# Earlier small loads, rearranged routing and no barrier around an untaken branch in a two-layer trunk on eight cores

## The reference, cut to what matters

```python
h = x * (1 + scale) + shift                      # rows of c @ ada_w + ada_b
x = layer_norm(alpha * x + (1 + gate) * mixer_or_moe(h), g, b)
# MoE
g_p, g_idx = top_k(softmax(h @ w_group + b_group), 1)
sel = expert_logits of group g_idx               # 8 per token
top_vals, top_idx = top_k(sel, 2)
w = softmax(top_vals) * g_p
y = sum over the two experts of w * (silu(h @ gate) * (h @ up)) @ down
```

## Time and profile before

| what | us |
|---|---|
| median of 3 runs | 2430.23 (2411.65, 2430.23, 2433.24) |
| profiled execution, its own time | 2433.36 |
| span of its slowest core (core 2) | 2432.3 |
| spans of the 8 cores | 2382.4 to 2432.3 |
| mean granted clock of TensorE, share of full | 0.77 to 0.78 |
| busy, core 2: PE, DVE, ACT, POOL | 1298.3, 1240.6, 640.7, 439.5 |
| DMA moved, core 2 | 413 MB |

### The profile page before, as it was taken

The page is one execution under the profiler, slowest core; times in us unless marked ns, Lnnn a source line. Parts: engine busy times, 40 slices in busy tenths (PEclk is TensorE's granted clock), DMA queues, the critical chain, the costliest instruction groups (busy, mean ns, idle before and its releaser), DMA issues.

```text
span 2432.3 us, 30523 instructions; the slowest of 8 cores (2382.4 to 2432.3 us)
## 1 busy us (share of the span) xinstructions
PE 1298.3 (53%) x9485; PEld 805.2 (33%) x9627; DVE 1240.6 (51%) x2415; ACT 640.7 (26%) x1257; POOL 439.5 (18%) x565
## 2 busy tenths in 40 slices
PE   0357767665064443645128878688840745556300
PEld 0134444443043322434014434344420534434200
DVE  2254565553255532453238667567633535555388
ACT  1234545443021111111013344244411311122000
POOL 2100102022131111110112212314012211111252
PEclk9678988787577767777569999889975867778655
DMA  9868986989899999799955888767855999999762
GB/s 182 144 107 130 105 114 102 117 102 112 102 186 240 213 249 221 153 246 225 228 116 76 156 155 148 123 132 125 137 147 158 195 253 244 271 246 267 263 204 104
DMA packets 92620, 413.13 MB, mean 170 GB/s; under 512 B 21223, under 2 KB 21223, under 8 KB 80617
## 3 DMA queue, kind: packets, MB, share of 16 engines
q0 software_dynamic: 41344, 211.43, 57.9%
q1 hardware_dynamic: 51102, 199.60, 24.8%
HBM read 454.49 MB, written 165.25 MB: 255 GB/s over the span
## 4 chain that ended last, share of the span: by engine, by line
DMA 38%; PE 20%; DVE 19%; issue 12%; ACT 4%; POOL 3%; SPq 3%; another core or an unknown queue 1%; DVEq 1%; ACTq 0%; POOLq 0%
DMA sb_W<-wb 8%; DMA sb_x<-xd 6%; DMA ys<-sb_hT 5%; PE bank L1288 4%; DMA sb_W<-ys,sb_idx 4%; DMA sb_hT<-xd 3%; SPq L347 2%; PE bank L1010 2%; DMA sb_W<-attn_w_qkv 2%; DMA xd<-sb_hT 2%; DVE sb_hT L1313 2%; DMA sb_A<-post_ln_b 2%; PE bank L1598 2%; DVE sb_x L1354 1%; PE bank L851 1%
## 5 line engine op out<-in xcount | busy, mean ns | idle before, releaser
L1288 PE MATMUL bank<-sb_hT,sb_W 128*128 128x256 bf16 x1984 | 306.4, 321 | 157.6 <-DMA sb_W<-wb 118.3
L1288 PEld LDWEIGHTS bank<-sb_hT,sb_W 128*128 128x128 bf16 x1984 | 221.5, 115 | 213.0 <-issue 161.2
L1270 ACT ACTIVATE sb_hT<-bank,sb_H 128x256 bf16<-128x256 f32 x256 | 130.4, 562 | 434.3 <-PE bank L1261 432.8
L1275 DVE TENSOR_SCALAR sb_hT<-bank,sb_H 128x256 bf16<-128x256 f32 x256 | 126.8, 537 | 188.2 <-PE bank L1261 162.9
L1313 DVE TENSOR_TENSOR sb_hT<-bank,sb_gtbf 128x512 f32<-128x512 f32 x176 | 121.5, 691 | 85.2 <-DMA ys<-sb_hT 66.4
L546 POOL TENSOR_TENSOR sb_rstdt<-sb_mvt,sb_eps_t 128x1 f32<-128x1 f32 x64 | 28.4, 444 | 638.5 <-DVE sb_mvt L542 284.3
L1598 PE MATMUL bank<-sb_W,sb_Z 128*128 128x512 bf16 x495 | 130.6, 410 | 1.5 <-issue 0.9
L1524 PE MATMUL bank<-sb_x,sb_Z 128*128 128x512 bf16 x488 | 122.1, 392 | 12.7 <-DVE sb_cact_rep L1579 9.2
L1261 PE MATMUL bank<-sb_ident,sb_hT 128*128 128x128 bf16 x512 | 49.3, 242 | 146.8 <-DMA sb_hT<-xh,sb_slots 88.3
L1309 PE MATMUL bank<-sb_W,sb_R 128*128 128x512 bf16 x436 | 113.0, 401 | 14.8 <-DVE sb_hT L1313 8.8
L1555 PE MATMUL bank<-sb_x,sb_Z 128*128 128x512 bf16 x508 | 120.6, 379 | 0.3
(11 more groups left out here) (249 smaller groups left out, 2699.1 us busy)
## 6 DMA issues: line engine op xcount, KB each, us to landing
wb<-moe_w POOLq DMA_DIRECT2D x41, 1536.0 KB, 21.9
sb_W<-wb SPq DMA_DIRECT2D x39, 1536.0 KB, 30.7
ys<-sb_hT SPq DMA_DIRECT2D x44, 1024.0 KB, 32.6
sb_W<-moe_w POOLq DMA_DIRECT2D x23, 1536.0 KB, 24.1
ys<-sb_Z SPq DMA_DIRECT2D x20, 1024.0 KB, 35.1
sb_A<-adaP POOLq DMA_DIRECT2D x30, 512.0 KB, 13.1
sb_x<-xin SPq DMA_DIRECT2D x16, 512.0 KB, 10.2
xd<-sb_x SPq DMA_DIRECT2D x16, 512.0 KB, 38.4
```

The costliest lines, as they stand in the source:

```text
L1270: S.op("act", (lambda k=k, src=src: lambda e: e.activation(out=hTe[i][:, k, :], in_=src, func=AF.Identity, scale=H1[haff][:, k:k + 1], bia ...
L1275: S.op("dve", (lambda k=k, src=src: lambda e: e.tensor_scalar(out=hTe[i][:, k, :], in0=src, scalar1=H1[haff][:, k:k + 1], scalar2=H0[haff] ...
L1288: S.op("pe", (lambda k=k, f=f, fc=fc: lambda e: e.matmul(banks[bk][:, f * 256:(f + 1) * 256], wgu[:, k, fc:fc + 128], hTe[i][:, k, :], sta ...
```

## The change

Five parts.

1. **Start.** The memsets of bqkv, kpad, Vaug and brr go to DVE, ahead. SP's order becomes pos, invf, adab0, rm, esink, xh, tokid, adabT, the clearing of `tab`, x0, x1; x2 to x5 wait for the first half of Wqkv. bqkv's DMA is the first of POOL's casting loads. The esink exponential comes behind the first eight chunks' consumption, X2k(-1) ahead of rope(0).
2. **Routing.** Groups of 4, 4, 4, 3 and 1 tiles. Both exponentials are one ACT instruction (`route_e`), run a tile later with b and c; the weights (`route_w`, DVE) a tile after that, with d. Within a step the order is d and w, then e, b and c, then a. `route_c` writes the slot index, then the flag, then the gather index, which has a buffer of its own.
3. **Attention loop.** job1 has a third step in every even t. The extra `moe_conv` is at t = 3, 5, 7 and 9. At the end of t = 14 job1 is drained and `make_aset(0)` runs; gtbf is loaded at t = 16.
4. **Barriers.** The barrier behind attention goes. In front of the branch each engine waits for the flag alone; the barriers are inside the branch, and behind it the buffer states of before are put back. `takes_over` lists stand where the barrier covered reuse of memory. Each layer has its flag.
5. **moe0_hook.** `affine` and the store of x run for tile e_-2; `make_aset(1)` and the load of gtbm at e_ = 18 instead of 17.

```diff
-    def region(self, name, flag):
-        self.barrier(own=True)
+    def region(self, name, flag, bflag):
+        for eng in self.ENG:
+            deps = {}
+            for p, v in bflag.w:
+                self._add_dep(deps, p, v)
...
         self.ops.append(("if", flag, (), None, 0))
         self.sfx = "_" + name
+        self.barrier(own=True)
...
+        GROUPS = [(0, 4), (4, 4), (8, 4), (12, 3), (15, 1)]
...
-            S.op("act", lambda e: e.activation(out=gex, in_=gex, func=AF.Exp), reads=[Brs], writes=[Brs])
-            vop(lambda e: e.tensor_reduce(out=gp, in_=gex, axis=AX.X, op=ALU.add))
-            vop(lambda e: e.reciprocal(out=gp, in_=gp))
...
+        def route_e(g):
+            v, _, _ = gw_views(g)
+            S.op("act", lambda e: e.activation(out=v, in_=v, func=AF.Exp), reads=[Bgw[g % 2]], writes=[Bgw[g % 2]])
...
-            for d, fn in ((0, route_a), (1, route_b), (1, route_c), (2, route_d)):
+            for d, fns in ((2, (route_d, route_w)), (1, (route_e, route_b, route_c)), (0, (route_a,))):
                 u = t - d
...
+            S.op("dve", lambda e: e.memset(bqkv[:], 0.0), writes=[Bbqkv])
+            S.op("dve", lambda e: e.memset(kpad[:], 0.0), writes=[Bkpad])
+            for i in range(3):
+                S.op("dve", (lambda i=i: lambda e: e.memset(Vaug[i][:], 1.0))(), writes=[BV[i]])
...
+            x_load(0); x_load(1)
+            dma("pool", "dw", bqkv[0:1, :], bqkv_d, writes=[Bbqkv])
             for n in range(8):
                 early_issue(n)
...
+            for t in range(2, 6):
+                S.op("sp", (lambda t=t: lambda e: e.dma_start(out=x[:, t, :], in_=xin[(t + 1) * 128:(t + 2) * 128, :]))(),
+                     reads=[BWqkv[0]], writes=[BX[t]], proc="dx")
...
                         if g == 1 and job1 is not None:
                             next(job1, None)
+                        if g == 3 and t % 2 == 0 and job1 is not None:
+                            next(job1, None)
...
-                    if t in (5, 10):
+                    if t in (3, 5, 7, 9):
                         moe_conv(0)
...
-                    route_step(t - 2)
-                for _ in job1:
-                    pass
-                takes_over([Bgtbf], [Bxb, Bborow])
-                bc_load(gtbf, Bgtbf, mod_d[3:4, :], reads=[Bmod[3]])
-                make_aset(0, None, None, None)
+                    route_step(t - 2, 0)
+                    if t == NT - 2:
+                        for _ in job1:
+                            pass
+                        make_aset(0, None, None, None)
+                    if t == NT:
+                        takes_over([Bgtbf], [Bxb, Bborow])
+                        bc_load(gtbf, Bgtbf, mod_d[3:4, :], reads=[Bmod[3]])
...
-            S.barrier()
...
-            if e_ < NT:
-                affine(e_)
-                dma("sp", "dx", xd_d[e_ * 128:(e_ + 1) * 128, :], x[:, e_, :], reads=[BX[e_]], writes=[Bxd[e_]])
-            if e_ == NT + 1:
+            t = e_ - 2
+            if 0 <= t < NT:
+                affine(t)
+                dma("sp", "dx", xd_d[t * 128:(t + 1) * 128, :], x[:, t, :], reads=[BX[t]], writes=[Bxd[t]])
+            if e_ == NT + 2:
```

More of the change, by code:

```diff
@@ L141, in barrier @@
                 self.ops.append((eng, None, waits, None, 0))
-    def region(self, name, flag):
-        self.barrier(own=True)
+    def region(self, name, flag, bflag):
[3 more added lines that the diff above has]
+                self._add_dep(deps, p, v)
+            waits = self._mk_waits(eng, deps)
+            if waits:
+                self.ops.append((eng, None, waits, None, 0))
+        self.kept = ({eng: dict(wd) for eng, wd in self.waited.items()},
+                     [(b, list(b.w), dict(b.r), list(b.pw), dict(b.pr)) for b in Buf.every])
         self.ops.append(("if", flag, (), None, 0))
         self.sfx = "_" + name
+        self.barrier(own=True)
     def region_end(self):
         self.barrier(own=True)
+        waited, bufs = self.kept
+        for eng, wd in self.waited.items():
+            for key in list(wd):
+                p = key[0] if isinstance(key, tuple) else key
+                if not p.endswith(self.sfx):
+                    if key in waited[eng]:
+                        wd[key] = waited[eng][key]
+                    else:
+                        del wd[key]
+        for b, w, r, pw, pr in bufs:
+            b.w, b.r, b.pw, b.pr = w, r, pw, pr
         self.sfx = ""
@@ L316, in build @@
         GT = 4
+        GROUPS = [(0, 4), (4, 4), (8, 4), (12, 3), (15, 1)]
+        gid = [g for g, (t0, n) in enumerate(GROUPS) for _ in range(n)]
+        NG = len(GROUPS)
         lg = carve(NT, 36)
@@ L366, in build @@
         S.op("dve", lambda e: e.memset(onesrow[:], 0.0), writes=[Bonesrow])
+        for l in range(2):
+            S.op("dve", (lambda l=l: lambda e: e.memset(brr[l][:], 0.0))(), writes=[Bwr[l]])
         S.op("dve", lambda e: e.memset(onesrow[0:1, :], 1.0), writes=[Bonesrow])
@@ L450, in route_a @@
                                           axis=AX.X, op=ALU.add))
[L451 to L456, removed]
+            argmax_onehot(sl, m1, o1, 8, rconst[:, 4:12], ot)
@@ L477, in route_b, with route_c @@
                  reads=[Butm, Bmaskb], writes=[PB[bk]])
-            S.op("pe", lambda e: e.matmul(banks[bk][:, 128:256], onesm[:], maskb16[:], start=True, stop=True),
+            S.op("pe", lambda e: e.matmul(banks[bk][:, 128:128 + n], onesm[:], maskb16[:, 0:n], start=True, stop=True),
                  reads=[Bonesm, Bmaskb], writes=[PB[bk]])
-        def route_c(g):
+        def route_c(g, l):
             bk = rt_bank[g]
-            ts = slice(g * GT, (g + 1) * GT)
-            for j in range(GT):
+            t0, n = GROUPS[g]
+            ts = slice(t0, t0 + n)
+            ps, rt, rk_, eb_, hi_ = pos[:, 0:n, :], rtmp[:, :, 0:n, :], rk[:, :, 0:n], eb[:, :, 0:n], hi2[:, :, 0:n]
+            for j in range(n):
@@ L519, in route_d @@
+            S.op("dve", lambda e: e.tensor_tensor(out=ix[:, 1, :, ts], in0=eb_, in1=v12[:, :, ts], op=ALU.mult),
+                 reads=[Bv12, Brs], writes=[Bidx2[g]])
         def route_d(g):
-            for t in range(g * GT, (g + 1) * GT):
+            t0, n = GROUPS[g]
+            for t in range(t0, t0 + n):
                 for k in range(2):
@@ L1046, in build @@
                     takes_over(BH[2 * n:2 * n + 2], [Bch_h[n]])
+                S.op("act", lambda e: e.activation(out=esink[:], in_=esink[:], func=AF.Exp), reads=[Besink], writes=[Besink])
                 pro_copy(-1); pro(-1)
```

200 lines of the change are left out of this document (117 added, 83 removed).

## The result

The changed kernel is slower: ratio to the kernel before 1.0098, 95% interval 1.0072 to 1.0123 (20 runs of each kernel, medians 2454.24 and 2431.88). Forecast was 2404, range 2350 to 2445.

A forecast was written before the change was run, and what follows sets the result against it. Attention mixed, MoE 0 bound by streamed weights, gMLP by PE and DVE order, passages by their chain. Terms -4 + 12 + 3 - 2 - 6 - 26 - 3 + 0 = -26: 2407.4 profiled, 2404 by median; range 2350 to 2445.

The forecast's parts named there:

- Start, -4: Before attention: early memsets remove PE's 21.30 wait, but the mod store holds the fold, at about 131.5 instead of 135.76.
- the upper bound: Start: +3, if the mod store begins its 16.4 at 116 and the fold comes at 139.
- Attention, +12 and +3: Attention loop: casts and chunks sooner cost +12, four pairs by 3; make_aset(0) at t = 14 and the drain +3.
- Two tiles then carry 3 x 12 + 5 x 4 = 56 against 53 for two tiles: Attention: casts at 12, chunks at 4, against two tiles' time; DMA falls behind by some 3 a pair.
- Routing, -2 and -6: One exponential replaces two DVE-ACT trips: -2 in attention, -6 in the gMLP, 2 in each of three groups.
- Passage into MoE 0, -26: Attention to MoE 0: only two scatters follow the flag, no A rows awaited; first T at 650.4 instead of 676.05.
- the bound of -12: Passage into MoE 0: scatters sit behind the weights' casting loads, or the slots load behind SP's xh store.
- MoE 0, -3: MoE 0: affine and stores of x leave the first two experts and run two longer at the other end.
- Second passage, 0: Passage into MoE 1: route_a delays logits by some 5, logits to last scatter takes 22.5 instead of 27; 0.
- C: Attention: casts cost more than 12, stopping PE in every pair; at 16 a cast +22, 2452; chance 0.13.
- B: MoE 0: DMA binds, two thirds of the passage's 26 given back waiting for weights; -9, 2421; chance 0.22.
- A: Start and attention: mod store lands early (-24), doubled tiles are absorbed (0); -58, 2372; chance 0.24.

The follow-up runs named there:

- e9: e3 with gate rows stored in 128 runs of 8, gate columns of ada_w and ada_b reordered ahead of launch; ratio to the kernel before 0.9659, median 2349.57.
- e2: Changed kernel with only the extra casts put back at t = 5 and 10; ratio to the kernel before 1.007.
- e3: Changed kernel with third job1 step, drain at t = 14 and make_aset(0) there undone, casts kept at 3, 5, 7, 9; ratio to the kernel before 0.9917.
- e1: Changed kernel with the whole of part 3, the attention loop's new order, undone; ratio to the kernel before 0.9894.
- e7: e3 with the gate row for the fold made on PE instead of stored to DRAM and loaded back; ratio to the kernel before 0.9865.
- e12: e9 with the barrier behind attention put back; ratio to the kernel before 0.9696.
- e10: Kernel before with only the store of gate rows in runs of 8; ratio to the kernel before 0.9919.
- e4: Kernel before with only part 3, the attention loop's new order, applied; ratio to the kernel before 1.0124.
- e11: Changed kernel with only the store of gate rows in runs of 8; ratio to the kernel before 0.9814.

## Why the prediction was wrong, point by point

- **Start, -4: +0.1.** What is late next was named rightly, and the upper bound was the better value. That the store would end "when the casting loads run dry" was the wrong picture: its single elements slowed the casting loads, which were still running at 127. The Trainium skill, page "DMA: Bandwidth & Descriptors", section "Rules for kernel authors", says that a last dimension that isn't contiguous goes out as one descriptor per element. The queue tables agree: where this store is SP's only transfer, queue 1 has 1040 packets (before, core 2, 112:127), and 144 with the store in 128 runs (e9, core 0, 83:91):

```profile
q1 hardware_dynamic: 1040, 0.00, 3.3%
```

```profile
q1 hardware_dynamic: 144, 0.00, 2.5%
```

- **Attention, +12 and +3: about +49 with routing.** This is the step that failed: "Two tiles then carry 3 x 12 + 5 x 4 = 56 against 53 for two tiles". First, 12 and 4 came from one stretch of 21.3 us. The DMA queue tables of 140:560 (before, then after) give more:

```profile
q0 software_dynamic: 5503, 37.83, 75.9%
q1 hardware_dynamic: 5902, 7.60, 6.9%
```

```profile
q0 software_dynamic: 7696, 40.53, 83.8%
```

  75.9% of 420 is 319 for 15 casts and 28 chunks, so, with a chunk as a third of a cast, an estimated 13.1 a cast and 4.4 a chunk; with SP's 6.9% of 53 a pair carries 39 + 22 + 4 = 65, 12 over 53 and not 3, 47 for four pairs. That this meets the 49 is luck. By the same sum e2 would lose 24 at most (two doubled pairs are left) and e3 some 30; against the kernel before their attention lost 51 and 11. So the balance of bytes against time, with whatever prices, is not what decides. Second, then, I priced moved work by its bytes and not by the distance between its issue and its use. A third step in every second tile uses each chunk, and the small row behind it, sooner after its issue; undoing the chunk part (e3) gives 38 back, the doubled casts cost 9. The runs show which edits cost it and which transfers are late; that the distance does it, and not the order in POOL's queue or the double cast of t = 5, was not tried by itself. The largest pieces by tile, against e3, are 9.5 at tile 4 (the small row, a DMA that I didn't list at all) and 13.3 at the step to tile 13 (A rows, for which I put 3).
- **Routing, -2 and -6.** In attention it isn't seen: parts 1, 2, 4 and 5 without part 3 (e1) make attention 2.7 longer. In the gMLP the two steps shrank by 1.4 and 1.8, some 3 a group. The stretch as a whole shows nothing: it moved by -7.1 to +2.1 in the runs with the new routing (without e7 and e12) and by -4.6 and +4.1 in e10 and e4, which have the old one.
- **Passage into MoE 0, -26: -21.8.** Each time of the chain came within 2.3 us of the forecast. Split at the last scatter (means of eight cores), the shorter row of scatters gives 6.5 of it (26.8 behind the logits before, 20.3 after) and the stretch from there to the first T 15.3 (29.6 before, 14.3 after). The first was forecast as 4.5. For the second the forecast had the A rows out of the way; the barriers have no part that can be seen (e12: 0.5). The runs show the last gate row's store of single elements behind it. That stretch is 15.4 with part 3 alone (e4), which lands this store ahead of the passage, and 14.8 with nothing changed but the store in runs (e10); it is 32.5 without part 3 (e1), where the store lands late again and the whole passage won only 3.7. That is the bound of -12 that I named, passed on the far side.
- **MoE 0, -3: -2.9. Second passage, 0: -7.4.** The first agreement shows little: e4 and e10, without part 5, took 491.1 and 485.6. In the second passage the delay of 5 by route_a ahead of the norm isn't seen; the shorter row of scatters is: the last one is issued 19.9 behind the logits instead of 28.0, and the first T comes 15.2 behind it instead of 14.6.
- **Rivals.** C (2452) is what happened in size and place, but not for its reason: it decides from 14.2 a cast, the estimate above is 13.1, and e2 loses as much with two doublings fewer. B, the gain ahead of MoE 0 given back there, is refuted: MoE 0 took 489 to 490 in the changed kernel, e1 and e3, and 487 in e9, whether its first T came at 606 or at 696. Its sign, over 100 of PE waiting for sb_W, came on some cores (71 to 113, mean 96.7; 86.5 before) without a longer stage. Of A, the early landing came in the changed kernel with another store (e11: fold at 103.6); the doubled tiles were not absorbed there (attention 421.4, 24 over the kernel before).

## What to carry to other kernels

When a step in a loop is moved ahead, list every DMA that it issues and how long after the issue each is used; a row of 4 KB among casts (39.12 to landing here) stops an engine as long as a large load. A wait that names one DMA can be due to an older one still in flight: look at what was issued before it and hasn't landed. A small transfer that can now be issued earlier may meet full DMA engines: look at how many separate pieces it has before counting on its idle duration. And where two covers lie over the same wait, removing one shows nothing; try both before calling an edit useless.

## What the runs showed of the hardware that was not expected

A store of 1024 single elements (4 KB) took 14.0 to 18.6 us alone and 40.0 to 44.1 among casting loads. While it ran, it took 3.2% of the engines' time itself, and a packet of the casting loads took 0.44 us of an engine instead of 0.29 to 0.30, at a busy share of 1.05 against 1.01 (before) and 1.05 (e9). In 128 runs of 8 it took 3.0 to 4.7 alone and 7.0 to 8.8 among the same loads. A full share in the table of stretches says nothing of how much is moved; the column behind it does.
